# A two-block transformer kernel on one core: shorter filler, GpSimd's squares behind VectorE's first low parts, column sums and spread of the first norm moved back

## The chip, the cores and the metric

The kernel runs on one core of one Trainium2 chip. The metric is the device time of one execution in microseconds (us). Engines: TensorE (PE, with its weight loads PEld), VectorE (DVE), ScalarE (ACT), GpSimd (POOL), and SyncE (SP), whose queue issues nearly all transfers.

## The reference

256 tokens of width 1024 pass through four layers in float32: a retention and pooling mixer, a conformer convolution, a gated short convolution, and sliding-window attention. Each is followed by a gated feed-forward block, and an RMS norm stands ahead of every part. Only the beginning matters here, the first norm and the first projection:

```python
def rms_norm(x, g):
    x32 = x.astype(jnp.float32)
    y = x32 * lax.rsqrt(jnp.mean(x32 * x32, axis=-1, keepdims=True) + EPS)
    return (y * g).astype(x.dtype)
...
def retention_pool_mixer(h, positions, w_in, ret_norm_g, pool_w, pool_scale, w_out):
    B, S, _ = h.shape
    proj = h @ w_in
    q, k, v, g, u = jnp.split(proj, [RET_WIDTH, 2 * RET_WIDTH, 3 * RET_WIDTH, 4 * RET_WIDTH], axis=-1)
...
def retention(q, k, v, positions):
    B, S, H, Dh = q.shape
    n_chunks = S // CHUNK
    q = rope(q, positions)
    k = rope(k, positions) * (Dh ** -0.5)
```

## The kernel before, in words

**Products in parts.** Activations lie transposed, as 8 tiles of 128 features by 256 tokens (`h`, k = 0 to 7). A float32 product is made of three: high weight by high x, high weight by low x, low weight by high x. ScalarE rounds the high parts (`xh` in `act_xh`, L345; `hi_t` in `early_hi` L307 and `split_hi` L318), VectorE subtracts for the low parts (`xl` in `dve_xl`, L349; `lo_t` in `early_lo` L311 and `split_lo` L324).

**Weights.** All weights are one stream of 2944 tiles of 128 x 128. 8 tiles are a piece, 2 pieces a chunk of 1 MB, which is one transfer into `raw_t` (3 slots). A slot is loaded again when both pieces of its chunk have their high and low parts (`load_chunk`, L263). `hi_t` and `lo_t` are rings of 6 pieces. `hi_to(e, c)` and `lo_to(e, c)` issue on ScalarE and VectorE every piece that is due by tile c of TensorE's order: piece n high parts from 8(n - 4) + 3 on, low parts from 8(n - 3) + 3 on. So `lo_to(e, 48)` ends with piece 8, `lo_to(e, 56)` with piece 9, and both `lo_to(e, 60)` and `lo_to(e, 64)` with piece 10. The semaphores `s_hi` and `s_lo` count pieces; the first four pieces are split by halves, one for each k, and `s_lo` is raised at every odd k, so it reaches 4 with the half of k = 7.

**The start.** SyncE issues the x tiles, the first four pieces, chunk 2 (pieces 4 and 5), then the tables (columns, positions, constants, pooling weights, and last the attention's sinks, `row`), then chunk 3 and so on. `pe_start` multiplies a matrix of ones `WARM_START` times into a bank that nothing reads; one such float32 product is 2 matmul records. `pe_first_tiles(e, k)` runs for k = 0 to 7 with 12 matmuls each (L787, L791, L795: high by high, high by low, low by high): tiles 0 to 31. Then `tile` (L393, L396, L399, in the same order of parts) takes tiles 32 to 63, piece by piece, and `strip` (L437, L440, L443) the values, tiles 64 to 95. `pe_retention` writes this order out by hand.

**The first norm** is applied after the products. GpSimd squares and adds the x tiles (`pool_start`): k = 0 directly into `ssum`, and for every further k a square (L743) and an add (L747). `pe_col_sums` (L454) sums over the features, `dve_mean` (L466) takes the mean, `pool_pow` (L473) the root on GpSimd, `dve_dg` (L479) puts it on a diagonal, `pe_spread` (L454) spreads it over the partitions and `dve_rbc` (L489) copies it out. It scales the rotation tables (L914, L915), with which queries and keys are rotated.

**VectorE's order at the start** (`dve_start`, then `dve_retention`): for each k `dve_xl` and `early_lo`; piece 4; a copy of the positions to float and three scalings (L712 to L719); a small product (L721); piece 5; four steps of the remainder of the angle (L726), and L728 to L733, the last two of which release ScalarE's sines; then, by `lo_to`, pieces 6 and on. ScalarE has its high parts up to piece 8 ahead of the sines (L873, L874), and piece 9 behind them.

Of the kernel before, what the change touches and what calls it, by code (L numbers as in the profile page):

```python
# [24 lines left out]
SCR = 12288  # L25
EARLY = 4
WIDE = 2
WARM_START = 21
N_RET = 5
N_CONF = 4  # L30
N_SHORT = 4
# [110 lines left out]
def rms_bank(i):  # L142
    return 2 if i % 2 or i == 2 else RMS_BANK
# [43 lines left out]
def model_kernel(nc, w, poolw, xT, pos, cols, rows, consts, shifts, out):  # L187
    ctx = ExitStack()
    with ctx:
# [3 lines left out]
        def sem(name):  # L193
            return ctx.enter_context(nc.semaphore(name))
# [32 lines left out]
        s_hi, s_lo, s_tiles = sem("hi"), sem("lo"), sem("tiles")  # L227
# [92 lines left out]
        def split_lo(e, p):  # L320
            if p >= RING:
                e.wait_ge(s_tiles, upto(8 * (p - RING) + 7))
            e.wait_ge(s_hi, p + 1)
            e.tensor_tensor(lo_t[:, p % RING, :], raw_of(p), hi_t[:, p % RING, :].bitcast(F32),  # L324
                            ALU.subtract).then_inc(s_lo, 1)
# [9 lines left out]
        def lo_to(e, c):  # L335
            while lo_next[0] < PIECES and 8 * (lo_next[0] - 3) + 3 <= c:
                split_lo(e, lo_next[0])
                lo_next[0] += 1
# [42 lines left out]
        def piece(e, g):  # L381
            p, r = divmod(g, 8)
            return p % RING, r

        def tile(e, g, dst, k, parts, first, last, arrives=None):

            slot, r = piece(e, g)
            c = slice(r * P, (r + 1) * P)
            if r == 0:
                e.wait_ge(s_hi, g // 8 + 1)  # L390
            if arrives:
                e.wait_ge(*arrives[0])
            e.matmul(dst, hi_t[:, slot, c], parts[:, k, 0, :], start=first, stop=False, skip_group_check=True)  # L393
            if arrives:
                e.wait_ge(*arrives[1])
            e.matmul(dst, hi_t[:, slot, c], parts[:, k, 1, :], start=False, stop=False, skip_group_check=True)  # L396
            if r == 0:
                e.wait_ge(s_lo, g // 8 + 1)
            m = e.matmul(dst, lo_t[:, slot, c], parts[:, k, 0, :], start=False, stop=last, skip_group_check=True)  # L399
            if g in MARKS:  # L400
                m.then_inc(s_tiles, 1)
# [51 lines left out]
        def plain(e, dst, lhs, rhs, start=True, stop=True):  # L453
            return e.matmul(dst, lhs, rhs, start=start, stop=stop, skip_group_check=True)  # L454

        def pe_col_sums(e, i):
            ps = banks[:, rms_bank(i), :]
            e.wait_ge(s_ssum, squares_in(i))
            for n, sums in enumerate((ssum, ssum2)[:2 if i == 4 else 1]):
                for a in range(2):  # L460
                    m = plain(e, ps[:, 2 * n + a:2 * n + a + 1], sums[:, a * P:(a + 1) * P], one[:, 0:1])
            m.then_inc(s_col_sums, 1)
# [18 lines left out]
        def pe_spread(e, i):  # L481
            n = 4 if i == 4 else 2
            e.wait_ge(s_dg, DG_AT[i] + n)
            plain(e, banks[:, rms_bank(i), 0:n * P], one[:, :],
                  dg4[:, 0:n, :].rearrange("p a b -> p (a b)")).then_inc(s_spread, 1)
# [198 lines left out]
        def pe_start(e):  # L684
            e.wait_ge(s_one, 1)
            for _ in range(WARM_START):
                plain(e, banks[:, RMS_BANK, 0:P], one[:, :], one[:, :])
# [47 lines left out]
        def pool_start(e):  # L735

            for k in range(KD):
                if k % 2 == 0:
                    e.wait_ge(s_x[k // 2], 16)
                if k == 0:  # L740
                    pl.mark(e.tensor_tensor(ssum[:, :], h[:, 0, :], h[:, 0, :], ALU.mult))
                    continue
                m = pl.mark(e.tensor_tensor(sq[:, k % 2, :], h[:, k, :], h[:, k, :], ALU.mult))  # L743
                e.wait_ge(pl.sem, m)
                if k > 1:
                    e.wait_ge(s_ssum, k - 1)
                e.tensor_tensor(ssum[:, :], ssum[:, :], sq[:, k % 2, :], ALU.add).then_inc(s_ssum, 1)  # L747
# [31 lines left out]
        def pe_first_tiles(e, k):  # L779

            half, at = k % 2, k // 2 + 1
            dsts = [banks[:, v, t * T:(t + 1) * T] for v in range(2) for t in range(2)]
            cols_of = [slice((4 * half + j) * P, (4 * half + j + 1) * P) for j in range(4)]
            e.wait_ge(s_hi if half else s_hi_half, at)
            e.wait_ge(s_xh, x_done(0, k))
            for j in range(4):
                e.matmul(dsts[j], hi_t[:, k // 2, cols_of[j]], x2[:, k, 0, :], start=k == 0 and j % 2 == 0, stop=False,  # L787
                         skip_group_check=True)
            e.wait_ge(s_xl, x_done(0, k))
            for j in range(4):  # L790
                e.matmul(dsts[j], hi_t[:, k // 2, cols_of[j]], x2[:, k, 1, :], start=False, stop=False,  # L791
                         skip_group_check=True)
            e.wait_ge(s_lo if half else s_lo_half, at)
            for j in range(4):
                m = e.matmul(dsts[j], lo_t[:, k // 2, cols_of[j]], x2[:, k, 0, :], start=False, stop=k == KD - 1,  # L795
                             skip_group_check=True)
            if half:
                m.then_inc(s_tiles, 1)

        def pe_retention(e):  # L800
            for k in range(KD):
                pe_first_tiles(e, k)
            for u in range(2, 4):
                for t in range(2):
                    for k in range(KD):
                        c = 16 * u + 8 * t + k
                        if c == 48:
                            pe_col_sums(e, 0)
                        if c == 60:
                            pe_spread(e, 0)  # L810
                        tile(e, G_QK + c, banks[:, u, t * T:(t + 1) * T], k, x2, k == 0, k == KD - 1)
            for k in range(KD):
                strip(e, G_V + 4 * k, (banks[:, 4, :], banks[:, 5, :]), k, k == 0, k == KD - 1)
            for u in range(2):
                e.wait_ge(s_qk, u + 1)
                for t in range(2):
                    for k in range(KD):
                        tile(e, G_U + 16 * u + 8 * t + k, banks[:, u, t * T:(t + 1) * T], k, x2, k == 0, k == KD - 1)
            for u in range(2):
                e.wait_ge(s_qk, u + 3)  # L820
                for t in range(2):
                    for k in range(KD):
                        c = 16 * u + 8 * t + k
                        tile(e, G_G + c, banks[:, 2 + u, t * T:(t + 1) * T], k, x2, k == 0, k == KD - 1)
                        if c % 8 == 3:
                            pe_head_scores(e, c // 8)
                        if c in (12, 24):
                            pe_pool(e, c // 24)

            for hd in range(4):  # L830
                e.wait_ge(s_sT, max(hd + 1, 3))
                m = plain(e, banks[:, 6, hd * P:(hd + 1) * P], sT[:, hd, 0:P], vt[:, 0, hd * P:(hd + 1) * P])
            m.then_inc(s_pv, 1)
            for hd in range(4):
                c = slice(hd * P, (hd + 1) * P)
                plain(e, banks[:, 7, c], sT[:, hd, P:T], vt[:, 0, c], True, False)
                m = plain(e, banks[:, 7, c], sT[:, hd, T:T + P], vt[:, 1, c], False, True)
            m.then_inc(s_pv, 1)
            e.wait_ge(s_g, 2)
            pe_out_blocks(e, 0, G_MO, N_RET, RET_ORDER, 0, 20)  # L840
            for pr in range(2):
                e.wait_ge(s_fl, f_done(0, 2 * pr + 1))
                for hd in (2 * pr, 2 * pr + 1):
                    for a in range(2):
                        e.wait_ge(s_on, a + 1)
                        m = e.transpose(banks[:, pr, (2 * (hd % 2) + a) * P:(2 * (hd % 2) + a + 1) * P],
                                        on[:, a, hd * P:(hd + 1) * P], ident)
                m.then_inc(s_turned, 1)
            pe_out_blocks(e, 0, G_MO, N_RET, RET_ORDER, 20, 40)
            pe_out_rest(e, 0, G_MO, N_RET, RET_ORDER)  # L850
# [53 lines left out]
                e.activation(fh[:, hd, :], oT[:, hd, :], ACT.Copy).then_inc(s_fh, 1)  # L904

        def dve_retention(e):
            lo_to(e, 48)
            dve_mean(e, 0)
            e.wait_ge(s_cst, 16)
            dve_dg(e, 0)  # L910
            lo_to(e, 60)
            dve_rbc(e, 0)
            e.wait_ge(s_sines, 1)
            e.tensor_tensor(cosr, cos, rbc[:, :], ALU.mult)  # L914
# [22 lines left out]
            for u in range(2):  # L937
                c = G_U + 16 * (u + 1)
# [1048 lines left out]
```

## Time and profile before

| | |
|---|---|
| median of 3 runs | 1133.82 us (1133.79 to 1134.82) |
| the profiled execution | 1137.05 us, its span 1135.3 us |
| TensorE busy | 1123.3 us, 99% of the span |
| VectorE busy | 833.4 us, 73% |
| ScalarE busy | 608.4 us, 54% |
| GpSimd busy | 44.6 us, 4% |
| granted TensorE clock, mean | 0.995 of full |

How to read it: the profile is one execution, recorded by the hardware. Times of a timeline count from the start of the span. Matmuls are pipelined, so a record is longer than the step to the next one; the pace is read from the starts. Idle time of an engine costs nothing unless the chain that ends last runs through it.

### The profile page before, as it was taken

To read this page: it belongs to the slowest core of one execution; us is meant where nothing else is said; L and a number is where in the kernel's file an instruction comes from. 1 tells how busy PE (TensorE), PEld (TensorE's weight loads), DVE (VectorE), ACT (ScalarE), POOL (GpSimd) and SP (SyncE) were. 2 spreads that over 40 slices of the span, in tenths; PEclk is the share of its full clock that TensorE was granted. 3 is DMA by queue.
4 is the path that set the end of the run, shared out by engine and by line. 5 is a ranking of instruction groups with operands and counts; after the bars stand their busy time and mean duration, and the time that the engine had idled before them with its cause. 6 is when DMAs were issued, how large, how long until landed. Compare 5 with 4: busy or idle time off the path is not lost.

```text
span 1135.3 us, 18825 instructions
## 1 busy us (share of the span) xinstructions
PE 1123.3 (99%) x7338; PEld 996.6 (88%) x7338; DVE 833.4 (73%) x1282; ACT 608.4 (54%) x951; POOL 44.6 (4%) x67
## 2 busy tenths in 40 slices
PE   9999999999999999999999999999999999999998
PEld 8999888888876988888899998888888789888887
DVE  7977877766774787777658867877665887877753
ACT  5646555544441656555453455655544667655631
POOL 4130000000000000000000000000001110000000
PEclk9999999999999999999999999999999999999999
DMA  8544555565484345555544645555554325555551
GB/s 308 191 152 180 186 186 186 185 211 172 161 268 138 108 157 211 193 187 190 205 163 151 221 149 186 189 189 189 213 186 153 144 76 180 186 192 186 191 186 68
DMA packets 35368, 203.53 MB, mean 179 GB/s; under 512 B 4176, under 2 KB 10576, under 8 KB 11984
## 3 DMA queue, kind: packets, MB, share of 16 engines
q1 hardware_dynamic: 35136, 202.32, 51.2%
q8 instruction: 58, 0.95, 0.3%
q14 instruction: 30, 0.25, 0.1%
q10 hardware_dynamic: 144, 0.01, 0.0%
HBM read 200.09 MB, written 2.23 MB: 178 GB/s over the span
## 4 chain that ended last, share of the span: by engine, by line
PE 93%; DVE 4%; issue 1%; ACT 1%; DMA 1%; SPq 0%; ACTq 0%; DVEq 0%
PE banks L415 44%; PE banks L421 23%; PE banks L393 6%; PE banks L399 5%; PE banks L396 5%; PE banks L454 5%; DVE lo_t L324 2%; PE banks L437 1%; PE banks L443 1%; PE banks L440 1%; DMA raw_t<-w 1%; DVE lo_t L311 0%; PE banks L1564 0%; ACT hi_t L318 0%; DVE x L349 0%
## 5 line engine op out<-in xcount | busy, mean ns | idle before, releaser
L324 DVE TENSOR_TENSOR lo_t<-raw_t,hi_t 128x1024 fp32r<-128x1024 f32 x364 | 439.5, 1218 | 7.5 <-ACT hi_t L318 6.3
L318 ACT ACTIVATE hi_t<-raw_t 128x1024 fp32r<-128x1024 f32 x364 | 376.0, 1049 | 68.2 <-DMA raw_t<-w 32.3
L415 PE MATMUL banks<-x,hi_t 128*128 128x512 f32 x1536 | 389.6, 394 | 0.5 <-DVE x L349 0.5
L415 PEld LDWEIGHTS banks<-x,hi_t 128*128 128x128 f32 x1536 | 275.4, 189 | 50.3 <-ACT x L345 0.9
L421 PEld LDWEIGHTS banks<-x,lo_t 128*128 128x128 f32 x1536 | 211.7, 190 | 16.5
L421 PE MATMUL banks<-x,lo_t 128*128 128x256 f32 x1536 | 216.6, 282 | 0.0
L415 PE MATMUL banks<-f,hi_t 128*128 128x512 f32 x704 | 181.3, 393 | 0.9 <-DVE f L539 0.9
L415 PEld LDWEIGHTS banks<-f,hi_t 128*128 128x128 f32 x704 | 124.8, 189 | 22.9 <-issue 2.5
L543 DVE TENSOR_TENSOR scr<-banks,scr 128x512 f32<-128x512 f32 x88 | 60.8, 691 | 84.4 <-ACT scr L595 83.7
L421 PEld LDWEIGHTS banks<-f,lo_t 128*128 128x128 f32 x704 | 99.3, 190 | 8.9
L421 PE MATMUL banks<-f,lo_t 128*128 128x256 f32 x704 | 101.8, 282 | 0.0
L393 PE MATMUL banks<-x,hi_t 128*128 128x256 f32 x288 | 82.9, 288 | 0.0
L595 ACT ACTIVATE scr<-banks 128x512 f32<-128x512 f32 x88 | 51.8, 593 | 57.3 <-PE banks L421 57.3
L399 PE MATMUL banks<-x,lo_t 128*128 128x256 f32 x288 | 81.7, 284 | 0.4 <-DVE lo_t L324 0.4
L396 PE MATMUL banks<-x,hi_t 128*128 128x256 f32 x288 | 81.5, 283 | 0.0
L589 ACT ACTIVATE f<-scr 128x256 fp32r<-128x256 f32 x88 | 36.8, 418 | 81.8 <-DVE scr L535 81.8
L573 DVE TENSOR_TENSOR h<-banks,h 128x256 f32<-128x256 f32 x32 | 13.6, 424 | 89.7 <-PE banks L421 89.7
L393 PE MATMUL banks<-f,hi_t 128*128 128x256 f32 x256 | 74.5, 291 | 0.8 <-issue 0.6
L396 PE MATMUL banks<-f,hi_t 128*128 128x256 f32 x256 | 73.0, 285 | 0.0
L399 PE MATMUL banks<-f,lo_t 128*128 128x256 f32 x256 | 72.9, 285 | 0.0
L345 ACT ACTIVATE x<-h,col 128x256 fp32r<-128x256 f32 x56 | 26.7, 503 | 84.3 <-DVE h L575 64.6
L609 ACT ACTIVATE scr<-scr 128x256 f32<-128x256 f32 x88 | 36.8, 418 | 62.2 <-DVE scr L559 62.2
(194 smaller groups left out, 1156.2 us busy)
## 6 DMA issues: line engine op xcount, KB each, us to landing
raw_t<-w SPq DMA_DIRECT2D x182, 1024.0 KB, 4.9
scr<-shifts SPq DMA_DIRECT2D x32, 142.0 KB, 3.6
raw_t<-w SPq DMA_DIRECT2D x3, 512.0 KB, 9.1
shifts<-scr SPq DMA_DIRECT2D x8, 144.0 KB, 3.6
h<-xT SPq DMA_DIRECT2D x4, 256.0 KB, 7.1
out<-h SPq DMA_DIRECT2D x8, 128.0 KB, 4.2
cst<-consts SPq DMA_DIRECT2D x1, 816.0 KB, 13.7
raw_t<-w SPq DMA_DIRECT2D x2, 256.0 KB, 5.4
```

What stands on the lines that cost most here:

```text
L318: e.activation(hi_t[:, p % RING, :], raw_of(p), ACT.Copy).then_inc(s_hi, 1)
L324: e.tensor_tensor(lo_t[:, p % RING, :], raw_of(p), hi_t[:, p % RING, :].bitcast(F32), ALU.subtract).then_inc(s_lo, 1)
L393: e.matmul(dst, hi_t[:, slot, c], parts[:, k, 0, :], start=first, stop=False, skip_group_check=True)
L396: e.matmul(dst, hi_t[:, slot, c], parts[:, k, 1, :], start=False, stop=False, skip_group_check=True)
L399: m = e.matmul(dst, lo_t[:, slot, c], parts[:, k, 0, :], start=False, stop=last, skip_group_check=True)
L415: e.matmul(halves(banks[:, to[j], :]), hi_t[:, slot, r * P:(r + 1) * P], parts[:, ks[j], :, :], start=ks[j] == 0, stop=False, skip_group_c ...
L421: m = e.matmul(banks[:, to[j], 0:T], lo_t[:, slot, r * P:(r + 1) * P], parts[:, ks[j], 0, :], start=False, stop=ks[j] == last_k, skip_grou ...
L454: return e.matmul(dst, lhs, rhs, start=start, stop=stop, skip_group_check=True)
L543: e.tensor_tensor(halves(t_ring[u % 3]), pair_of(u, 0), halves(b_ring[u % 2]), ALU.add).then_inc(s_up, 1)
L589: e.activation(fh[:, u, :], m_ring[u % 2], ACT.Copy).then_inc(s_fh, 1)
L595: e.activation(halves(b_ring[u % 2]), pair_of(u, 1), ACT.Copy).then_inc(s_side, 1)
L609: e.activation(s_ring[u % 2], t_ring[u % 3][:, 0:T], ACT.Silu).then_inc(s_silu, 1)
```

## The change

- `WARM_START` goes from 21 to 18 products of ones.
- In `pool_start`, GpSimd waits ahead of the square of k = 2 until `s_lo` is 4 (`EARLY`), that is, until VectorE has the low part of the weights of k = 7. Squares of k = 2 to 7 and their adds lie behind this wait; the square of k = 0 and the square and add of k = 1 stay ahead of it.
- In `pe_retention`, the column sums come ahead of tile 56 instead of tile 48, and the spread behind tile 63 instead of ahead of tile 60.
- In `dve_retention`, the mean comes behind `lo_to(e, 56)` instead of `lo_to(e, 48)`, so piece 9 goes ahead of it; the copy of the spread root comes behind `lo_to(e, 64)` instead of `lo_to(e, 60)`, which issue the same pieces.

```diff
--- before.py
+++ after.py
@@ -25,7 +25,7 @@
 SCR = 12288
 EARLY = 4
 WIDE = 2
-WARM_START = 21
+WARM_START = 18
 N_RET = 5
 N_CONF = 4
 N_SHORT = 4
@@ -737,6 +737,9 @@
             for k in range(KD):
                 if k % 2 == 0:
                     e.wait_ge(s_x[k // 2], 16)
+                if k == 2:
+
+                    e.wait_ge(s_lo, EARLY)
                 if k == 0:
                     pl.mark(e.tensor_tensor(ssum[:, :], h[:, 0, :], h[:, 0, :], ALU.mult))
                     continue
@@ -804,11 +807,10 @@
                 for t in range(2):
                     for k in range(KD):
                         c = 16 * u + 8 * t + k
-                        if c == 48:
+                        if c == 56:
                             pe_col_sums(e, 0)
-                        if c == 60:
-                            pe_spread(e, 0)
                         tile(e, G_QK + c, banks[:, u, t * T:(t + 1) * T], k, x2, k == 0, k == KD - 1)
+            pe_spread(e, 0)
             for k in range(KD):
                 strip(e, G_V + 4 * k, (banks[:, 4, :], banks[:, 5, :]), k, k == 0, k == KD - 1)
             for u in range(2):
@@ -904,11 +906,11 @@
                 e.activation(fh[:, hd, :], oT[:, hd, :], ACT.Copy).then_inc(s_fh, 1)
 
         def dve_retention(e):
-            lo_to(e, 48)
+            lo_to(e, 56)
             dve_mean(e, 0)
             e.wait_ge(s_cst, 16)
             dve_dg(e, 0)
-            lo_to(e, 60)
+            lo_to(e, 64)
             dve_rbc(e, 0)
             e.wait_ge(s_sines, 1)
             e.tensor_tensor(cosr, cos, rbc[:, :], ALU.mult)
```

## Rows read from the trace of the kernel before

**Rows 1.** The page: the chain that ended last, share by engine.

```profile
PE 93%; DVE 4%; issue 1%; ACT 1%; DMA 1%; SPq 0%; ACTq 0%; DVEq 0%
```

**Rows 2.** Timeline of TensorE, 0 to 35 us: start, length, instructions [idle before].

```profile
1.04 7.24 PE L454 MATMUL banks<-one 128*128 128x128 f32 x42 [1.04 <-DVE one L706]
8.03 0.71 PE L787 MATMUL banks<-x,hi_t 128*128 128x256 f32 x4
...
21.16 0.28 PE L393 MATMUL banks<-x,hi_t 128*128 128x256 f32 x1
...
27.33 0.50 PE L454 MATMUL banks<-one,ssum 128*128 128x1 f32 x4
...
28.42 0.38 PE L399 MATMUL banks<-x,lo_t 128*128 128x256 f32 x1 [0.25 <-DVE lo_t L324]
28.64 0.28 PE L393 MATMUL banks<-x,hi_t 128*128 128x256 f32 x1
...
32.23 0.28 PE L393 MATMUL banks<-x,hi_t 128*128 128x256 f32 x1
...
34.45 0.40 PE L437 MATMUL banks<-hi_t,x 128*128 128x512 f32 x1
```

**Rows 3.** Timeline of VectorE, 9 to 32 us.

```profile
9.27 0.48 DVE L349 SCALAR_TENSOR_TENSOR x<-h,col,x 128x256 fp32r<-128x256 f32 x1 [0.54 <-ACT x L345]
...
17.96 1.10 DVE L311 TENSOR_TENSOR lo_t<-raw_t,hi_t 128x512 fp32r<-128x512 f32 x1
18.98 0.95 DVE L349 SCALAR_TENSOR_TENSOR x<-h,col,x 128x256 fp32r<-128x256 f32 x1
19.85 0.68 DVE L311 TENSOR_TENSOR lo_t<-raw_t,hi_t 128x512 fp32r<-128x512 f32 x1
20.45 1.21 DVE L324 TENSOR_TENSOR lo_t<-raw_t,hi_t 128x1024 fp32r<-128x1024 f32 x1
...
22.37 0.29 DVE L717 TENSOR_SCALAR scr<-scr 128x256 f32<-128x256 f32 x1
...
24.12 1.79 DVE L726 SCALAR_TENSOR_TENSOR scr<-scr 128x256 f32<-128x256 f32 x4
...
27.14 3.49 DVE L324 TENSOR_TENSOR lo_t<-raw_t,hi_t 128x1024 fp32r<-128x1024 f32 x3
30.55 0.15 DVE L466 TENSOR_SCALAR st<-banks 128x2 f32<-128x2 f32 x1
31.60 0.48 DVE L479 TENSOR_SCALAR dg<-cst,st 128x128 f32<-128x128 f32 x2 [0.89 <-POOL st L473]
```

**Rows 4.** Timeline of GpSimd, 4 to 20 us.

```profile
4.96 0.61 POOL L741 TENSOR_TENSOR ssum<-h 128x256 f32<-128x256 f32 x1 [4.12 <-DMA h<-xT]
5.54 0.61 POOL L743 TENSOR_TENSOR sq<-h 128x256 f32<-128x256 f32 x1
6.22 0.79 POOL L747 TENSOR_TENSOR ssum<-ssum,sq 128x256 f32<-128x256 f32 x1
...
18.59 1.06 POOL L747 TENSOR_TENSOR ssum<-ssum,sq 128x256 f32<-128x256 f32 x1
```

**Rows 5.** Filler matmuls, early and late: count, min/median/max ns, first and last start.

```profile
L454 PE MATMUL banks<-one x14: 421/421/580, 1.0 to 4.0; 128*128 128x128 f32 x14
...
L454 PE MATMUL banks<-one x17: 275/275/275, 6.2 to 8.0; 128*128 128x128 f32 x17
```

**Rows 6.** Timeline of ScalarE, 15 to 33 us.

```profile
15.97 0.62 ACT L307 ACTIVATE hi_t<-raw_t 128x512 fp32r<-128x512 f32 x1
17.59 2.01 ACT L318 ACTIVATE hi_t<-raw_t 128x1024 fp32r<-128x1024 f32 x2 [0.99 <-DMA raw_t<-w]
24.95 2.01 ACT L318 ACTIVATE hi_t<-raw_t 128x1024 fp32r<-128x1024 f32 x2 [5.36 <-DMA raw_t<-w]
...
30.37 1.99 ACT L318 ACTIVATE hi_t<-raw_t 128x1024 fp32r<-128x1024 f32 x2
```

**Rows 7.** Transfers issued from 5 to 14 us: count, KB, median us to landing.

```profile
row<-rows SPq DMA_DIRECT2D x1, 8.0 KB, 13.2
```

## The prediction

> **What bounds the kernel now.** The reader begins with the chain that ended last: 93% of it is TensorE [rows 1]. So a time changes only if TensorE reaches some product earlier or later and nothing behind it gives that back. The change touches the first 35 us, so the next view is TensorE's timeline there [rows 2]: filler from 1.04, the first real products at 8.03, tile 32 at 21.16, and from then on a steady 0.36 us a tile (ten tiles from 28.64 to 32.23). Two places in it matter. At tile 48 the third matmul starts at 28.42, after 0.25 us of idle that ended with VectorE's low part of piece 6. And tile 64, the first strip, starts at 34.45; the strips and all that follows run from there. I take 34.45 as the finish line: behind it no edit touches TensorE, and the weights are split well ahead.
>
> Then VectorE's timeline [rows 3], and GpSimd's beside it [rows 4]. The low part of piece 6 comes at 27.14, as the end of a chain without idle: low part of piece 4 at 20.45, the angle arithmetic with piece 5 in it, then pieces 6 to 8. Up to 20.45 this chain is stretched. A low x part takes 0.48 us at 9.27 but 0.95 at 18.98, a half-piece low part 0.68 at 19.85 but 1.10 at 17.96; one round lasts 1.89 us (17.96 to 19.85) where the starts of undisturbed operations would give 0.60 + 0.43 = 1.03. GpSimd is stretched with it (0.61 us against 1.06). Both together look like one at a time on something shared: 1.89 = 1.03 + two GpSimd operations at 0.43. I call 0.43 us the hold of one GpSimd operation.
>
> **The change, part by part.**
> Filler: 3 products fewer are 6 matmuls. Late filler matmuls start every 0.11 us (17 from 6.2 to 8.0), early ones every 0.23 (14 from 1.0 to 4.0) [rows 5]. The last ones go, so 6 x 0.107 = 0.64 us; TensorE begins its tiles at 7.39. The granted clock's row reads full throughout, but the durations, 421 ns against 275 ns, show that the faster pace has long begun by then, so I charge nothing for it.
>
> GpSimd's wait: squares 2 to 7 with their adds, 12 operations, wait for the low part of k = 7. Queued behind on GpSimd are only a memset and the power of the root, wanted far later. Column sums need the seventh add. VectorE's first parts now run at their own pace and meet the high parts of ScalarE, whose last starts at 15.97 - 0.62 long, so over at 16.59 [rows 6]. The low part of k = 7 then runs from 16.74 to 17.43 instead of ending at 20.53, and TensorE, with 96 matmuls at 0.12 us (a third of a tile's 0.36) and 0.3 us put down for waits on ScalarE, goes from 7.39 to tile 32 at about 19.24, 1.9 us sooner. But the high part of piece 4 is there only at 18.65 (its transfer lets ScalarE begin at 17.59 [rows 6]), so VectorE takes piece 4 at 18.68: its chain gains 1.77 us, not 3.1.
>
> Now the 12 operations are repaid. GpSimd starts at 17.50 and slips two of them in before 18.68. Ten are left, beside a chain that had no company before. The end of this part is bounded thus. Nothing lost: 27.14 - 1.77 = 25.37, but then the high part of piece 6 (24.95 + 1.05 = 26.0, set by its transfer) decides, and its low part ends at 27.2. All ten paid in full: 25.37 + 4.3 + 1.22 = 30.9. Between them I step through the chain. An operation of VectorE that finds GpSimd in a hold waits for its end and the other way round; GpSimd wants back in about 0.26 us after a square and 0.15 us after an add (alone, its starts are 0.68 and 0.58 apart [rows 4], less the hold of 0.43). This gives: piece 4 18.68 to 19.82, square 3 to 20.25, the integer copy, add 3 at 20.51, the scalings each pushed back by 0.1 to 0.35, piece 5 from 23.04 to 24.18, the four steps of the remainder with a GpSimd operation before each (24.61, 25.38, 26.15, 26.92), the last add 27.26 to 27.69, the angles by 28.89. Piece 6 then runs 28.89 to 30.11, against 28.36 now: 1.75 us later. TensorE, waiting 0.4 us at tile 32 and 1.4 at tile 40, stands at tile 48 from 27.3 on and starts its third matmul at 30.17 instead of 28.42.
>
> Whether the single-input operations in this chain (the copy, six scalings and clamps) wait for GpSimd no row shows, since none of them runs beside it. One of them does 256 elements in 0.29 us [rows 3], the two-input step in 1.79 / 4 = 0.45: it moves two elements at a time, which I take to mean that it uses the same second way in. If they don't wait, the same stepping ends piece 6 at 28.35, as today.
> The Trainium skill, SBUF — State Buffer, section "Who interferes with whom", says that a VectorE instruction with two SBUF inputs, and also a copy, cast or tensor_scalar in a two-port mode, shares a port pair with GpSimd, held for the whole instruction. The doubled rows agree for two inputs; for the single-input ones no row here shows it, and it would give the 30.11.
>
> Column sums: they move behind tile 55. Today their record is 0.50 us long at 27.33 [rows 2], but inside a stretch that ends with a wait for piece 6 and so is free. Later nothing waits around them: I charge 0.4, a record less the overlap of a tenth that neighbouring records have. Spread: moved from tile 60 to 64; the 15 tiles from 28.64 fill 5.39 of the 5.81 us to 34.45, so it costs 0.42, paid once either way. VectorE's piece 9 now goes before the mean. Its high part is over at 31.4 (30.37 plus 1.05), behind ScalarE's sines, so low part 31.45 to 32.58, mean, and 1.05 us from the mean to the first diagonal (30.55 to 31.60), 0.48 more to the end of the second: 34.11. TensorE would come to the spread at 27.26 + 0.22 (28.42 to 28.64) + 5.39 + 0.4 = 33.27 at the very best, and would wait; with piece 6 at 30.11 it comes at 36.18 and doesn't. Root and rotation tables slip by about 2 us with it; their first user on TensorE is ten microseconds further on.
> Transfers: slots are freed earlier, but the 8 KB of sinks, landed 13.2 us after their issue behind all the rest [rows 7], show a queue served in turn, backed up by more than ten microseconds; chunk 3, behind them, can't land sooner, and 26.0 stands.
>
> **The sum.** 1.75 + 0.40 = 2.15 us later at the strips (36.60). The profiled execution took 1137.05 us with a span of 1135.3; it would take 1139.2. The median of the runs is 1133.82, three microseconds less; the edit is a fixed cost at the start, so I add it there: 1136.0.
>
> **Rivals.**
> A. Single-input operations ignore GpSimd. For it: no row shows the contrary. Then piece 6 is where it was and only the column sums are paid: 34.45 + 0.40, so 1134.2.
> B. The squares cost VectorE next to nothing in their new place. Then piece 6 ends at 27.2, TensorE is quick, and the spread's diagonals (34.11) decide: strips at 34.15 + 0.42 = 34.57, plus 0.1 us: 1133.9. The doubled durations speak against it.
> C. Faster: the gained start reaches the end. It needs piece 6 and the diagonals to be early too, so a faster ScalarE and an earlier transfer. If the whole of tile 32's lead survived: minus 1.9 us, 1131.9. Against it: both are set by rows that the change leaves alone.
> D. Clearly slower: the wait at tile 48 (27.3 to 30.17, with 1.8 us of idle shortly before) makes TensorE fall to its slow pace. Matmuls then run at half pace for as long as at the start, from 1.04 to about 5.7, a loss of 2.3 us more: 1138.3. It decides only if the wait passes roughly what I forecast. No row shows a wait of three microseconds in a dense stretch here. The Trainium skill (TensorE: Matmul & The Clock Gate, "Why this matters for your kernels") warns of idle gaps over about 3 us; mine is 2.9.
>
> **How the numbers follow.** Forecast 0.55, A 0.2, B 0.1, C 0.03, D 0.08, something else 0.04. The forecast's own spread is about 0.7 us each way, from the order in which the two engines win. Measurements tell 0.2%, 2.27 us, from no change. Forecast's 2.15 lies just inside: 0.25 of its 0.55 is taken to lie beyond, and with D and a rest 0.33 slower; faster 0.04; the same 0.63. Range 1133.6 to 1137.2: it holds A, B and the forecast, and leaves out C and D.
>
> **What would show it.** Each step has its mark in the new profile: tiles beginning at 7.4; VectorE's first parts at 0.48 and 0.69; piece 4 near 18.7; GpSimd's squares from 17.5 to 28; the scalings stretched from 0.29 to 0.5 and more (if not: A); TensorE's third matmul of tile 48 near 30.2 after a wait of nearly 3 us; strips near 36.6; filler-like long matmuls after the wait would be D. I am wrong if piece 6 is ready before 28.

## The result, and the profile after

The changed kernel takes 1138.05 us (median, 1136.71 to 1140.88), the kernel before, measured beside it, 1134.58 us (1133.79 to 1134.92): ratio 1.0036, 95% interval 1.0023 to 1.0049. That is 3.5 us slower. The forecast was 2.15 us, added to an earlier median of 1133.82: 1136.0 us. The time lies above the range.

The profiled execution took 1137.89 us, its span is 1136.1 us. Read with [rows 2], TensorE's timeline to 40 us shows the loss and where it begins (start, length, instructions, idle before and what ended it):

```profile
7.74 0.71 PE L790 MATMUL banks<-x,hi_t 128*128 128x256 f32 x4
...
25.61 0.39 PE L399 MATMUL banks<-x,lo_t 128*128 128x256 f32 x1 [1.37 <-DVE lo_t L324]
...
31.73 0.39 PE L399 MATMUL banks<-x,lo_t 128*128 128x256 f32 x1 [2.99 <-DVE lo_t L324]
...
34.47 0.50 PE L454 MATMUL banks<-one,ssum 128*128 128x1 f32 x4
...
38.45 0.39 PE L440 MATMUL banks<-hi_t,x 128*128 128x512 f32 x1
```

The first tiles begin 0.3 us sooner than before (7.74). On its way to tile 32 TensorE stands 0.81 us for a high part from ScalarE (at 14.73). Then at tile 40 it waits 1.37 us and at tile 48 another 2.99 us, these two for the low part of a piece from VectorE. The third matmul of tile 48 starts at 31.73, before at 28.42 [rows 2]: 3.31 us later. The column sums (34.47) lie in dense work now. The second matmul of the first strip starts at 38.45; in the trace of before it starts at 34.68. So the strips are 3.77 us late, and nothing behind them gives that back.

Why piece 6 is late stands in VectorE's timeline, to be read against [rows 3]:

```profile
17.32 0.48 DVE L349 SCALAR_TENSOR_TENSOR x<-h,col,x 128x256 fp32r<-128x256 f32 x1
...
19.58 1.48 DVE L324 TENSOR_TENSOR lo_t<-raw_t,hi_t 128x1024 fp32r<-128x1024 f32 x1 [1.18 <-ACT hi_t L318]
20.98 0.70 DVE L712 CAST scr<-scr 128x256 f32<-128x256 int32 x1
21.79 0.70 DVE L715 TENSOR_SCALAR scr<-scr,col 128x256 f32<-128x256 f32 x1
22.52 0.59 DVE L717 TENSOR_SCALAR scr<-scr 128x256 f32<-128x256 f32 x1
23.14 0.78 DVE L719 TENSOR_SCALAR scr<-scr 128x256 f32<-128x256 f32 x1
...
24.35 1.21 DVE L324 TENSOR_TENSOR lo_t<-raw_t,hi_t 128x1024 fp32r<-128x1024 f32 x1
25.48 3.34 DVE L726 SCALAR_TENSOR_TENSOR scr<-scr 128x256 f32<-128x256 f32 x4
...
30.26 0.28 DVE L733 TENSOR_SCALAR scr<-scr 128x256 f32<-128x256 f32 x1
30.46 4.62 DVE L324 TENSOR_TENSOR lo_t<-raw_t,hi_t 128x1024 fp32r<-128x1024 f32 x4
```

The first parts do what the change wants: 0.48 us for a low x part (17.32) where it was 0.95. Then the chain: piece 4 begins at 19.58, 0.87 us sooner than before; piece 6 at 30.46, 3.32 us later. Everything between is stretched. The copy (L712) takes 0.70 us in place of 0.28, the scalings 0.59 to 0.78 in place of 0.29 (0.35 for L715), the four steps together 3.34 in place of 1.79. The last one (L733, 30.26), behind GpSimd's last add, has its 0.28 again. GpSimd's timeline is the other half, to be read against [rows 4]:

```profile
18.54 0.61 POOL L746 TENSOR_TENSOR sq<-h 128x256 f32<-128x256 f32 x1 [11.77 <-DVE lo_t L311]
...
19.93 1.59 POOL L746 TENSOR_TENSOR sq<-h 128x256 f32<-128x256 f32 x1
...
22.30 0.66 POOL L746 TENSOR_TENSOR sq<-h 128x256 f32<-128x256 f32 x1
...
24.48 1.67 POOL L750 TENSOR_TENSOR ssum<-ssum,sq 128x256 f32<-128x256 f32 x1
...
28.62 0.78 POOL L750 TENSOR_TENSOR ssum<-ssum,sq 128x256 f32<-128x256 f32 x1
```

Squares and adds now run from 18.54 to 29.40. An operation that meets a whole piece on VectorE is stretched most: 1.59 us at 19.93, beside piece 4, and 1.67 at 24.48, beside piece 5. With nobody beside them the first is a square of 0.61 us and the second an add of 0.73 to 0.79. Both engines wait for each other, one operation at a time.

ScalarE's timeline, against [rows 6], has the third part:

```profile
18.48 2.01 ACT L318 ACTIVATE hi_t<-raw_t 128x1024 fp32r<-128x1024 f32 x2 [0.96 <-DMA raw_t<-w]
25.24 2.01 ACT L318 ACTIVATE hi_t<-raw_t 128x1024 fp32r<-128x1024 f32 x2 [4.75 <-DMA raw_t<-w]
...
31.30 1.99 ACT L318 ACTIVATE hi_t<-raw_t 128x1024 fp32r<-128x1024 f32 x2
```

The transfer of piece 4 lets ScalarE begin at 18.48, before at 17.59.

The two profiled executions differ by only 0.84 us (1137.89 against 1137.05), though the strips are 3.77 us late. The execution profiled of before was a long one for its kernel, 2.5 us above its median, and the windows say where. Of after, then of before (window, busy time and instructions of each engine, granted clock, DMA share, GB/s):

```profile
357.00:361.00 4.00, 1.73 (x36) 0.94 (x28) 1.29 (x3) 0.42 (x1) 0.00 (x0) 1.00 0.95 230
367.00:371.00 4.00, 3.74 (x33) 3.49 (x30) 2.03 (x9) 1.90 (x3) 0.69 (x1) 1.00 0.00 0
917.00:921.00 4.00, 4.00 (x26) 3.47 (x24) 3.58 (x7) 2.00 (x6) 0.00 (x0) 0.63 0.63 244
```

```profile
357.00:361.00 4.00, 4.00 (x49) 2.63 (x44) 0.00 (x0) 0.00 (x0) 0.00 (x0) 0.57 0.82 275
367.00:371.00 4.00, 3.74 (x16) 3.19 (x15) 1.81 (x9) 0.44 (x2) 0.69 (x1) 0.58 0.00 0
917.00:921.00 4.00, 4.00 (x27) 3.59 (x26) 2.79 (x5) 1.60 (x6) 0.00 (x0) 0.57 0.44 182
```

Before met three stretches of 3.4 us at half the full clock, after only the last of them. Two such falls at about 1.5 us each (worked out with e2_wait_only below) are what the profile of before has too much. They lie far behind the edits. So the comparison goes by medians, and below, where the clock of each execution is on record, by executions with the same mean clock.

### The profile page after: what moved, and what is told of

The parts are those of the page before. It is cut to its first block, busy times and chain, and to the rows that moved or that the text cites. A ratio compares the mean times of both kernels' runs of the same rounds, so it can differ in the third digit from the quotient of the medians.

```text
span 1136.1 us, 18814 instructions
## 1 busy us (share of the span) xinstructions
PE 1119.5 (99%) x7332; PEld 993.7 (87%) x7332; DVE 833.6 (73%) x1282; ACT 608.6 (54%) x951; POOL 44.8 (4%) x67
## 4 chain that ended last, share of the span: by engine, by line
PE 93%; DVE 4%; DMA 1%; issue 1%; ACT 1%; SPq 0%; DVEq 0%; ACTq 0%
PE banks L415 44%; PE banks L421 23%; PE banks L393 6%; PE banks L399 5%; PE banks L396 5%; PE banks L454 5%; DVE lo_t L324 2%; PE banks L437 1%; PE banks L443 1%; PE banks L440 1%; DMA raw_t<-w 1%; ACT hi_t L318 1%; PE banks L1566 0%; PE banks L1552 0%; DVE scr L726 0%
```

## The experiments

The theory, P: VectorE and GpSimd take turns on something that they share; GpSimd's twelve operations were moved from a stretch in which VectorE waits anyway into a chain in which it never does. Rivals: F, the shorter filler with its idle and clock; S, the later column sums and spread; W, TensorE's long wait makes it fall to its slow pace. The table gathers the profiled execution of each (us): where ScalarE can begin piece 4, where VectorE begins the low parts of pieces 4 and 6, TensorE's third matmul of tile 48, and its second of the first strip.

| kernel | piece 4 there | low 4 | low 6 | chain (6 less 4) | tile 48 | strips |
|---|---|---|---|---|---|---|
| before | 17.59 | 20.45 | 27.14 | 6.69 | 28.42 | 34.68 |
| after | 18.48 | 19.58 | 30.46 | 10.88 | 31.73 | 38.45 |
| e1_no_wait | 18.45 | 20.63 | 27.34 | 6.71 | 28.61 | 35.99 |
| e2_wait_only | 19.04 | 20.13 | 30.45 | 10.32 | 31.72 | 39.47 |
| e3_filler_only | 18.03 | 20.40 | 27.10 | 6.70 | 28.37 | 34.63 |
| e4_sums_only | 17.82 | 20.39 | 27.09 | 6.70 | 28.36 | 35.24 |
| e5_no_squares | 18.19 | 19.28 | 26.00 | 6.72 | 27.27 | 34.84 |
| e6_wait_at_6 | 17.64 | 18.73 | 27.06 | 8.33 | 28.34 | 35.05 |
| e7_fill_the_wait | 17.23 | 18.32 | 29.33 | 11.01 | 30.60 | 37.30 |
| e8_scalar_squares | 18.63 | 19.72 | 26.43 | 6.71 | 27.70 | 37.82 |

The mean granted clock of every execution is on record too, and it roughly counts falls: one stretch of 3.4 us at half clock in 1135 us leaves a mean of 0.998, none leaves 1.000. So executions with the same mean can be compared without their falls (mean of the times, us, number of executions in brackets; before is what was measured beside the experiments, after was measured at another time):

| kernel | at 0.998 | at 1.000 |
|---|---|---|
| before | 1134.34 (32) | 1132.60 (9) |
| after | 1137.58 (3) | none |
| e1_no_wait | 1135.10 (6) | 1133.56 (1) |
| e2_wait_only | 1137.46 (3) | none |
| e3_filler_only | 1134.04 (3) | 1132.72 (3) |
| e4_sums_only | 1135.09 (4) | 1133.42 (5) |
| e5_no_squares | 1134.51 (5) | 1133.03 (6) |
| e6_wait_at_6 | 1134.82 (7) | 1133.32 (4) |
| e7_fill_the_wait | 1137.94 (4) | 1136.83 (1) |
| e8_scalar_squares | 1137.17 (6) | none |

After is 3.24 us above before at the same mean clock, with as many falls.

**e1_no_wait**, against the changed kernel:

```diff
                if k % 2 == 0:
                    e.wait_ge(s_x[k // 2], 16)
-               if k == 2:
-                   e.wait_ge(s_lo, EARLY)
```

> The changed kernel with GpSimd's new wait taken out again: 18 filler products and the later column sums and spread stay. Theory P (the twelve squares and adds, moved beside VectorE's chain without idle, delay the low part of piece 6): the chain is as before, third matmul of tile 48 near 28.4 us, only the column sums (0.4 us) are paid, median +0.2 to +0.8 us against the kernel before. Rival F (the start with less filler, idle and clock, costs the time): still +2 us or more. Rival S (the later sums and spread cost it): still +2 us or more.

Measured: ratio 1.0011, interval 1.0002 to 1.0020, median 1135.21 us against 1134.26. Nearly three quarters of the loss are gone, and tile 48's third matmul is back at 28.61. What is left, 0.95 us, is a little above the 0.2 to 0.8 expected, and more than the column sums alone. TensorE's timeline:

```profile
28.61 0.39 PE L399 MATMUL banks<-x,lo_t 128*128 128x256 f32 x1 [0.70 <-DVE lo_t L324]
...
35.23 0.70 PE L454 MATMUL banks<-dg,one 128*128 128x256 f32 x2 [0.41 <-DVE dg L479]
```

It stands 0.41 us for the diagonals ahead of the strips. Pieces 8 and 9 landed late in this execution, piece 9 had no high part before 32.4, and the mean is queued behind its low part.

**e2_wait_only**, against the kernel before:

```diff
                if k % 2 == 0:
                    e.wait_ge(s_x[k // 2], 16)
+               if k == 2:
+                   e.wait_ge(s_lo, EARLY)
```

> The kernel before with nothing but GpSimd's wait ahead of the square of k = 2. Theory P: the whole loss less the column sums, which disappear in the wait: low part of piece 6 about 3 us later, VectorE's single-input operations at 0.6 to 0.7 us in place of 0.29, median +2.5 to +3.5 us. Rivals F and S: below +0.7 us.

Measured: ratio 1.0036, interval 1.0024 to 1.0049, median 1137.57 us, 3.3 above before: practically the whole loss by this line alone. F and S fall as its cause. VectorE's timeline has the same marks:

```profile
20.13 1.61 DVE L324 TENSOR_TENSOR lo_t<-raw_t,hi_t 128x1024 fp32r<-128x1024 f32 x1 [2.44 <-ACT hi_t L318]
21.66 0.70 DVE L712 CAST scr<-scr 128x256 f32<-128x256 int32 x1
...
30.25 0.29 DVE L733 TENSOR_SCALAR scr<-scr 128x256 f32<-128x256 f32 x1
30.45 3.49 DVE L324 TENSOR_TENSOR lo_t<-raw_t,hi_t 128x1024 fp32r<-128x1024 f32 x3
```

This execution, the longest of the kernel (1140.45 us), shows rival W at work too. TensorE had waited 1.14, 1.37 and 1.85 us by 31.7; its windows (busy time, granted clock, DMA share, GB/s):

```profile
30.00:33.00 3.00, 1.28 (x10) 1.00 0.17 71
33.00:36.00 3.00, 3.00 (x17) 0.51 0.71 205
36.00:38.00 2.00, 2.00 (x15) 0.88 0.86 270
38.00:40.00 2.00, 2.00 (x16) 1.00 0.87 336
```

From 33.0 to 36.4 matmuls start every 0.21 us in place of 0.12, so the granted clock of 0.51 is the lower level, 1.2 GHz. The strips come 7.75 us behind tile 48's third matmul (31.72 to 39.47), against 6.26 before (28.42 to 34.68): a fall costs 1.5 us. The changed kernel waited 1.37 us (at tile 40) and then 2.99 in its profile, and kept 1.00. The Trainium skill (TensorE: Matmul & The Clock Gate, "Why this matters for your kernels") warns of idle gaps over about 3 us; here the fall came behind gaps of at most 1.85 us, and none came behind one of 2.99. What decides it these runs don't show (see also e8_scalar_squares).

**e3_filler_only**, against the kernel before:

```diff
-WARM_START = 21
+WARM_START = 18
```

> The kernel before with 18 filler products in place of 21. Theory P: TensorE's first tiles begin about 0.5 us sooner and wait that much more for VectorE's first parts and for piece 6; median within 0.4 us of before. Rival F: +1 us or more, with slow matmuls (421 ns filler, long first tiles) or a longer idle after the filler.

Measured: ratio 1.0002, interval 0.9993 to 1.0011, median 1134.14 us against 1134.26. Tile 48 and the strips stand where they stood (28.37, 34.63). TensorE's lead of 0.3 us at the start (first tiles at 7.70) is waited away: 0.61 us at 14.30 for a high part of ScalarE, and from 17.16 on TensorE waits for VectorE's low parts as before.

**e5_no_squares**, against the changed kernel:

```diff
-            for k in range(KD):
+            for k in range(2):
                 if k % 2 == 0:
                     e.wait_ge(s_x[k // 2], 16)
-                if k == 2:
-                    e.wait_ge(s_lo, EARLY)
...
-                e.tensor_tensor(ssum[:, :], ssum[:, :], sq[:, k % 2, :], ALU.add).then_inc(s_ssum, 1)
+                e.tensor_tensor(ssum[:, :], ssum[:, :], sq[:, k % 2, :], ALU.add).then_inc(s_ssum, 7)
```

The kernel leaves out the squares of k = 2 to 7, and its one add raises the semaphore by 7, so that nothing waits for the missing ones.

> The changed kernel with GpSimd's squares and adds of k = 2 to 7 left out altogether (the norm is then that of the first 256 features only). Nobody is beside VectorE. Theory P: first parts at 0.48 and 0.69 us, scalings at 0.29, low part of piece 6 over by 27.2 to 27.6, set by its transfer; strips then wait for the diagonals (near 34.1), so they start at about 34.6, median -0.3 to +0.5 us against before. If the diagonals don't bind, down to -0.7 us. Rivals F and S: +2 us or more, as in the changed kernel.

Measured: ratio 0.9996, interval 0.9988 to 1.0005, median 1133.31 us against 1134.26. The median is lower than expected because 6 of its 11 executions had no fall of the clock; at the same mean clock it is 0.2 and 0.4 us above before. All of VectorE's chain has its own pace (6.72 us), and piece 6's low part begins at 26.00, 1.14 us before its old place. Yet the time isn't below that of before:

```profile
27.27 0.39 PE L399 MATMUL banks<-x,lo_t 128*128 128x256 f32 x1 [0.69 <-DVE lo_t L324]
...
34.07 0.70 PE L454 MATMUL banks<-dg,one 128*128 128x256 f32 x2 [0.59 <-DVE dg L479]
```

Tile 48 gained 1.15 us; then the column sums are paid and TensorE stands 0.59 us for the diagonals ahead of the spread. The diagonals are the next thing late, as worked out in the prediction (34.11, here 34.0).

**e4_sums_only**: the changed kernel's column sums, spread, mean and copy of the root, on the kernel before:

```diff
-                        if c == 48:
+                        if c == 56:
                             pe_col_sums(e, 0)
-                        if c == 60:
-                            pe_spread(e, 0)
                         tile(e, G_QK + c, banks[:, u, t * T:(t + 1) * T], k, x2, k == 0, k == KD - 1)
+            pe_spread(e, 0)
...
-            lo_to(e, 48)
+            lo_to(e, 56)
             dve_mean(e, 0)
```

> The kernel before with only the column sums and the spread (and VectorE's mean and copy with them) moved; 21 filler products, GpSimd free to run at once. Theory P: the part is worth the column sums that are no longer hidden, 0.4 us, plus whatever the diagonals come too late: strips start 0.4 to 1.2 us later than before, according to when the transfer of pieces 8 and 9 lands, median +0.3 to +1.3 us. Rival (the part is free, its price in the undo run was chance): within 0.2 us.

Measured: ratio 1.0002, interval 0.9994 to 1.0011, median 1134.92 against 1134.32. The traces say +0.56 us at the strips (35.24 against 34.68). The ratio can't tell that from nothing; the executions with the same mean clock do, with +0.75 us at 0.998 and +0.82 at 1.000. That is all of what e1_no_wait kept (+0.76), so the part isn't free.

**e6_wait_at_6**, against the changed kernel:

```diff
-                if k == 2:
+                if k == 6:
                     e.wait_ge(s_lo, EARLY)
```

> The changed kernel with GpSimd's wait ahead of the square of k = 6 in place of k = 2: 4 operations stay behind the wait in place of 12. Theory P, one at a time at about 0.41 us: two of the four slip in before piece 4, two are paid, the chain starts earlier than before by 1 to 1.5 us, so piece 6's low part begins at 26.0 to 27.3 and the loss of 3.3 us at tile 48 is gone altogether, not to a third; strips as in the run without the wait, median +0.2 to +1.3 us. If instead the wait itself costs (whatever lies behind it): still +2.5 us or more. If the cost goes by operations moved in proportion: about +1.5 us over the run without the wait.

Measured: ratio 1.0000, interval 0.9991 to 1.0009, median 1134.39 us against 1134.32. A third of the operations moved, and none of the loss at tile 48; the later column sums are still paid (+0.48 us at the same mean clock of 0.998, +0.37 at the strips). VectorE's and GpSimd's timelines:

```profile
18.73 1.59 DVE L324 TENSOR_TENSOR lo_t<-raw_t,hi_t 128x1024 fp32r<-128x1024 f32 x1 [0.26 <-ACT hi_t L318]
20.24 0.82 DVE L712 CAST scr<-scr 128x256 f32<-128x256 int32 x1
...
22.61 0.29 DVE L719 TENSOR_SCALAR scr<-scr 128x256 f32<-128x256 f32 x1
...
27.06 3.49 DVE L324 TENSOR_TENSOR lo_t<-raw_t,hi_t 128x1024 fp32r<-128x1024 f32 x3
```

```profile
18.62 0.61 POOL L746 TENSOR_TENSOR sq<-h 128x256 f32<-128x256 f32 x1 [3.02 <-DVE lo_t L311]
19.31 1.59 POOL L750 TENSOR_TENSOR ssum<-ssum,sq 128x256 f32<-128x256 f32 x1
20.86 0.66 POOL L746 TENSOR_TENSOR sq<-h 128x256 f32<-128x256 f32 x1
21.61 0.74 POOL L750 TENSOR_TENSOR ssum<-ssum,sq 128x256 f32<-128x256 f32 x1
```

Here the exchange can be read to the end. Two of the four operations were expected to slip in ahead of piece 4; none did, the first begins 0.11 us ahead of it. Piece 4 begins at 18.73, 1.72 us sooner than before; the four operations stretch the chain by 8.33 - 6.69 = 1.64 us, 0.41 each; piece 6 begins at 27.06, where it always did. For four operations, what the early stretch gives back is what the late one costs. VectorE already stands 0.26 us for ScalarE there, so piece 4 can't come sooner, and more operations moved should bring nothing more and cost 0.41 us each: eight more make 3.3, as in the changed kernel. Only four and twelve were run; the steps between are inferred.

**e7_fill_the_wait**, against the changed kernel:

```diff
+                        if c == 48:
+                            for _ in range(10):
+                                plain(e, banks[:, RMS_BANK, 0:P], one[:, :], one[:, :])
                         if c == 56:
                             pe_col_sums(e, 0)
```

> The changed kernel with 10 products of ones put ahead of tile 48, into the wait for piece 6, so that TensorE isn't idle there for three microseconds. If the wait alone costs: median as the changed kernel, +3.3 us or up to 0.3 more, and the long ones among its runs (1139 to 1141) go away. If TensorE's fall to the slow pace behind the wait is part of the usual cost: 0.5 us or more below the changed kernel's +3.5.

Measured: ratio 1.0032, interval 1.0021 to 1.0043, median 1138.18 us against 1134.32, so 3.9 us where 3.3 to 3.6 was expected. The wait is filled and the loss stays:

```profile
27.12 2.39 PE L454 MATMUL banks<-one 128*128 128x128 f32 x20
...
30.60 0.38 PE L399 MATMUL banks<-x,lo_t 128*128 128x256 f32 x1 [0.85 <-DVE lo_t L324]
```

So the wait itself is the usual loss. The record of the clocks says the same of W: at a mean clock of 0.998 four executions of this kernel take 1137.94 us and three of the changed kernel 1137.58, both more than 3 us above before with as many falls. Its longest run is 1139.52 us where the changed kernel's is 1140.88; whether the filling removes falls of the clock is not settled by so few.

**e8_scalar_squares**, an attempt at a better kernel, against the kernel before:

```diff
             for p in range(EARLY, RING):
                 split_hi(e, p)
+            for k in range(2, KD):
+                e.activation(early_sq(k), h[:, k, :], ACT.Square).then_inc(s_early, 1)
...
+                if k > 1:
+                    if k == 2:
+                        e.wait_ge(s_angle, 2)
+                        e.wait_ge(s_early, KD - 2)
+                    e.wait_ge(s_ssum, k - 1)
+                    e.tensor_tensor(ssum[:, :], ssum[:, :], early_sq(k), ALU.add).then_inc(s_ssum, 1)
+                    continue
...
-                        if c == 48:
+                        if c == 60:
                             pe_col_sums(e, 0)
-                        if c == 60:
-                            pe_spread(e, 0)
...
+            pe_spread(e, 0)
```

> The kernel before with the squares of k = 2 to 7 on ScalarE, in its wait for chunk 3, and GpSimd's six adds behind the angles; column sums at tile 60, spread at the strips, mean still ahead of piece 9. Theory P: VectorE's first parts and its chain have nobody beside them (0.48, 0.69, 0.29 us), piece 6's low part is set by its transfer and over by 27.3 to 27.8, tile 48 gains 0.6 to 1.1 us, 0.4 of it go to the column sums: median -0.1 to -0.8 us. If adds beside pieces 6 to 8 delay tile 48 or the mean: 0 to +0.8 us.

Measured: ratio 1.0031, interval 1.0020 to 1.0042, a miss. Half of the expectation held: tile 48's third matmul comes at 27.70, 0.72 us sooner. But I had reckoned the six adds at their own length. TensorE's and GpSimd's timelines:

```profile
27.70 0.39 PE L399 MATMUL banks<-x,lo_t 128*128 128x256 f32 x1 [0.69 <-DVE lo_t L324]
...
34.14 0.60 PE L454 MATMUL banks<-one,ssum 128*128 128x1 f32 x4 [2.11 <-POOL ssum L753]
```

```profile
26.65 7.44 POOL L753 TENSOR_TENSOR ssum<-ssum,scr 128x256 f32<-128x256 f32 x6 [19.23 <-DVE scr L738]
```

Beside pieces 6 to 8, each of which holds the shared way for about 1.13 us (the step from one low part of a piece to the next operation), the adds take 7.44 / 6 = 1.24 us apiece and end at 34.09. TensorE waits 2.11 us for them ahead of the column sums. The sharing goes both ways.

The wait isn't all that this execution (1139.63 us) paid. Behind it TensorE's clock fell, as in e2_wait_only's profile: from 35.5 to 39.1 its matmuls run at half pace, and the window says so (busy time, granted clock, DMA share, GB/s):

```profile
36.00:38.00 2.00, 2.00 (x8) 0.50 0.01 4
```

TensorE's gaps up to then were 0.76 us (at 21.0), 0.69 (at 27.7) and 2.11. Six of the nine executions have the mean clock of a single fall and still take 2.8 us more than before, so the fall isn't the usual loss here either.

## Why the prediction was wrong, point by point

**The mechanism held.** The finish line (nothing behind the strips gives the loss back), the taking of turns, the first parts at 0.48 and 0.69 us, waits of nearly 3 us at tile 48 (2.9 forecast, 2.99 measured) and of 1.4 us at tile 40 (1.37), the column sums at 0.4 (tile 48 late by 3.31, strips by 3.77: 0.46), the diagonals that bind when piece 6 is early: all in the traces. The wait at tile 48 has the forecast length, but both of its ends lie 1.4 to 1.6 us later than forecast (27.3 to 30.17, in the trace 28.7 to 31.73), since pieces 5 and 6 are late alike. e2_wait_only shows that the wait alone makes the loss, e5_no_squares that the operations behind it do.

**Rival A is out.** The single-input operations wait too: 0.70 us in place of 0.28 for the copy beside GpSimd, 0.59 to 0.78 for scalings where L733 takes 0.28 once GpSimd is done. The Trainium skill, SBUF — State Buffer, "Who interferes with whom", says that a copy, cast or tensor_scalar in a two-port mode contends with GpSimd, and these rows agree.

**The step that failed is a term of the sum:** piece 6 later by 1.75 us; it was 3.32. It was mis-sized in two places: in when the chain starts, and in what GpSimd's operations cost it.

First, the transfer. I took the high part of piece 4 to be ready at 18.65 because one execution had it so. In the ten profiled executions ScalarE began piece 4 between 17.23 and 19.04 us, and in the changed kernel's at 18.48, 0.89 later than in before's. In the kernel before that moment is covered: VectorE comes to piece 4 only at 20.45. In the changed kernel nothing covers it, and each tenth goes into the chain. That was 0.90 of the missing 1.57 us here. e7_fill_the_wait had its piece 4 at 17.23, earlier than I assumed, and is still 2.18 us late at tile 48.

Second, the turns. I stepped through the chain and charged it 3.52 us for ten operations, taking the short operations of VectorE to slip into GpSimd's gaps. Measured, the chain is 10.88 - 6.69 = 4.19 us longer. The copy and the scalings took 0.42, 0.35, 0.30 and 0.49 more, the small product 0.41, the four steps 1.55 and L728 0.41: ten operations, 0.39 each, with nothing slipped in for free. The other 0.26 is on piece 4, from an eleventh operation: the add of k = 2 was still running when piece 4 was due, where I had it done. The upper bound, 4.3, was close to the right value, and was in the text; that it had ten operations and not eleven is luck. That is the other 0.67 us.

**Filler.** 3 products fewer were to bring tiles 0.64 us sooner; it was 0.3, since the matmuls of 421 ns, which ended by 5.7 us in before's trace, lasted to 6.4 in after's. Nor did TensorE reach tile 32 at 19.24 but at 20.59, with 0.81 us of waiting for ScalarE where 0.3 was put down. Neither matters, since the low parts of pieces 5 and 6 decide; e3_filler_only shows it for the filler.

**The range** ended at 1137.2. Beside the two terms it stood on 1133.82, the median of before then; beside the changed kernel it was 1134.58. With both terms at their measured sizes the sum is 1134.58 + 3.32 + 0.46 = 1138.4, against 1138.05.

**Rival D** happened, in an execution of e2_wait_only and in one of e8_scalar_squares, for 1.5 us in the first rather than the 2.3 estimated. It isn't the usual loss: the changed kernel's profile has the full clock there, and executions with the same mean clock differ by the whole 3.2 us. That its 1138.3 us lies next to the measured 1138.05 is chance.

**Open:** how often the changed kernel's clock falls behind its wait. Its times spread over 4.2 us (1136.71 to 1140.88), but so do those of before where it was measured most often (1132.06 to 1136.02). Its two longest, 1139.33 and 1140.88, have mean clocks of 0.997 and 0.996, so about one fall more, or two, than the three executions at 0.998; where they lay no trace shows. None of its six has 1.000, against 9 of before's 54.

## What to carry to other kernels

Work that is taken off one engine's path by moving it behind a wait has to be charged where it lands: ask of both stretches whether the neighbour on the shared way in has idle time of its own. In the old place twelve operations at 0.41 us delayed piece 4 by 0.9 to 1.8 us (20.45, where its transfer allowed 18.7 to 19.6), because VectorE waited for transfers anyway; in the new one eleven of them cost 4.19. And an event that the old kernel covers (here a transfer) must enter the sum with its spread over executions as soon as the change uncovers it, for which a single trace gives one value only.

## What the runs showed of the hardware that was not expected

- VectorE and GpSimd take turns, whatever the length of the operations: an operation of GpSimd costs VectorE 0.39 us (after, mean of ten) to 0.41 (e6_wait_at_6, mean of four), and a low part of a whole piece holds up GpSimd's square or add until it takes 1.24 to 1.67 us in place of 0.61 to 0.79.
- The landing of a 1 MB transfer in a backed-up queue, read from when ScalarE could begin piece 4, moved by 1.8 us between executions of ten nearly equal programs (17.23 to 19.04).
- The moment at which TensorE's filler goes from 421 ns to 275 ns moved too, between 5.7 us (before) and 6.4 us (after) from the start of the span.
- TensorE's clock fell to its lower level for 3.4 us behind a gap of 1.85 us (e2_wait_only, after two of 1.14 and 1.37) and behind one of 2.11 (e8_scalar_squares), and not behind one of 2.99 (after). Falls also come far from any edit: three in the profile of before. One costs 1.5 to 1.7 us (e2_wait_only's strips; 1134.34 against 1132.60 us for before with and without one).
